# Two experts at a time: a large and a small one take turns step by step, with a down product between gate and up

## The chip, the cores and the metric

The program runs on one core of one Trainium2 chip. The metric is device time in microseconds: the median of the kernel before is 1894.28 us over three runs (1891.65 to 1898.52). The core works with TensorE (matmuls), VectorE and ScalarE (elementwise work), GpSimd, and SyncE, which issues the loads from HBM. Each engine takes its own list of instructions in order; they wait for each other by semaphores.

## The reference, cut to what matters

Two transformer blocks over 256 tokens of width 1024. The last stage, where the change is, is a mixture of experts: a router picks 2 of 8 experts for each token, and every expert is a gated product with an inner width of 3584.

```python
logits = (hf @ w_router)
top_val, top_idx = lax.top_k(logits, 2)
gates = jax.nn.softmax(top_val, axis=-1)
...
def expert_block(args):
    xb, e = args
    return (jax.nn.silu(xb @ w_gate[e]) * (xb @ w_up[e])) @ w_down[e]
...
h = layer_norm(ALPHA * h + y, ln_g, ln_b)
```

Everything is float32, and the products keep nearly all of that accuracy.

## The kernel before, in words

A float32 product is made of products of a faster 4-byte format. Each weight is cut into a high part (ScalarE copies it into `WHB` or `WHX`, line 1290) and the rest (VectorE subtracts, into `WLB` or `WLX`, line 1911). The rows are cut the same way. An expert with up to 128 tokens ("large") needs three matmuls for each pair of tiles: high by high, high by low, low by high (`mm3`, lines 442 to 444). For an expert with at most 64 tokens ("small", `LIGHT`) high and low rows stand side by side in one operand of 128 columns, so two matmuls do (lines 1093 and 1094, 1139 and 1140); its two halves are then added when the hidden rows are turned (`expert_turn`, line 1117: 16 small matmuls, where a large expert has 4).

The experts are ranked by their load, and the table `RANK` says which rank stands at which position. Before, positions 0, 3 and 6 are large and the others small, and one expert is done after the other.

The weights of one expert are 21 loads of 2 MB: for each of its seven chunks of 512 inner columns one of gate, up and down. SyncE issues them in the order of the list `WL_M`, into four slots (three of `ring`, and `ring4`); a slot is loaded again once VectorE has cut its contents. Each load is cut in two halves ("pieces"), 42 an expert. The cut parts have four places. ScalarE cuts four pieces ahead of TensorE (`split_to(done + 3)`, line 1276) and VectorE three ahead (line 1904); the fourth place comes free only when TensorE has used up the piece in it. In between, the same two engines take the results from PSUM, at fixed points of their lists.

The seven chunks are done in steps of one or two (`steps_of`, line 38). A step is, on TensorE: gate products of this step's chunks; after their first piece the turn of the first chunk of the step before; up products, and among them the turn of its second chunk; then the down products of the chunks of the step before. PSUM banks are fixed: gate in 0 and 1, up in 2 and 3, down in 4 and 5, the turn in 6, all else in 7 (`LAST_BANK` for the last sums). Among these stand the gathering of the next expert's rows (`gather`, line 1056), its lists (`scatter_lists`) and the sums of the last expert into the tokens' rows (`combine`, line 1175). After the last expert come its sums, a layer norm (lines 2650 and 2655) and the stores.

Of the kernel before, what the change touches and what calls it, by code (L numbers as in the profile page):

```python
# [8 lines left out]
F32 = mybir.dt.float32  # L9
# [23 lines left out]
RANK = (0, 3, 4, 1, 5, 6, 2, 7)  # L33
LIGHT = (1, 2, 4, 5, 7)
# [88 lines left out]
def build(nc, I, table, out):  # L123
    ctx = ExitStack()
    with ctx:
# [16 lines left out]
        VS = sb("VS", [128, 256])  # L142
# [3 lines left out]
        BC = sb("BC", [128, 2, D])  # L146
        NG = sb("NG", [128, 128])
        GM = sb("GM", [128, 2, 64])
        LAMB = sb("LAMB", [128, 256])
# [20 lines left out]
        with ExitStack() as part:  # L170
# [18 lines left out]
            CT2 = pt("CT2", [128, 192])  # L189
        P8 = ctx.enter_context(nc.psum_tensor("PS", [128, 4096], F32))  # L190
# [33 lines left out]
        T = {}  # L224
# [46 lines left out]
        for ex in range(NE):  # L271
            for cs in steps_of(ex):
                for kind in ("gate", "up"):
                    if len(cs) == 2:
                        WL_M += [(f"{kind} {ex}", (CH * cs[0], 4 * k), None, 4, 2 * CH) for k in range(2)]
                    else:
                        WL_M.append((f"{kind} {ex}", (CH * cs[0], 0), None, 8, CH))
                WL_M += held
                held = [(f"down {ex}", 4 * c, None, 4, D) for c in cs]
# [144 lines left out]
        def pe_program(e):  # L424
# [631 lines left out]
            def gather(ex, q):  # L1056

                pe.wait_ge(s_po, ex + 1)
                light = ex in LIGHT
                for n, src in enumerate((HH, HL)):  # L1060
                    pe.wait_ge(*((s_hl, 2) if n else (s_hh, 2)))
                    b = 6 + (q if light else n)
                    if not (light and n):
                        room(b)
                    for j in range(4):
                        d = 4 * q + j
                        for tt in range(2):
                            if light:
                                at_ = 128 * j + 64 * n
                                t = e.matmul(PS[b][:, at_:at_ + 64], src[:, tt, 128 * d:128 * d + 128], PO[:, tt, 0:64], start=(tt == 0), stop=(tt == 1))  # L1070
                            else:
                                t = e.matmul(PS[b][:, 128 * j:128 * j + CAP], src[:, tt, 128 * d:128 * d + 128], PO[:, tt, :], start=(tt == 0), stop=(tt == 1))  # L1072
                    if n or not light:
                        t.then_inc(banks.put(("ga", ex, q, n), b), 1)

            def expert_piece(kind, ex, cs, k):
# [3 lines left out]
                at_ = 0 if kind == "gate" else 2  # L1080
# [4 lines left out]
                for j in range(n_kt):  # L1085
                    kt = n_kt * k + j
                    for x, c in enumerate(cs):
                        b = at_ + (NCH * ex + c) % 2
# [3 lines left out]
                        if ex in LIGHT:  # L1092
                            e.matmul(PS[b][:, :], EH[:, kt, :], wh, start=(kt == 0), stop=False)  # L1093
                            t = e.matmul(PS[b][:, :], EH[:, kt, :], wl, start=False, stop=(kt == 7))  # L1094
# [3 lines left out]
                if k == 2 * len(cs) - 1:  # L1098
                    for c in cs:
                        banks.put((kind, ex, c), at_ + (NCH * ex + c) % 2, full=used)  # L1100
# [6 lines left out]
            def expert_turn(ex, c):  # L1107
                n = NCH * ex + c
                i = n % 2
                room(6)  # L1110
                if ex in LIGHT:
                    pe.wait_ge(s_tab2, 16)
                    for x, (kind, src) in enumerate((("gate", HID[:, i, :]), ("up", UB[:, :]))):
                        pe.wait_ge(*banks.out[kind, ex, c])
                        for j in range(4):
                            at_ = 256 * x + 64 * j
                            t = e.matmul(PS[6][:, at_:at_ + 64], inner(src, j), CT2[:, 128:192], start=True, stop=True)
                else:
                    pe.wait_ge(*banks.out["up", ex, c])
                    for j in range(4):  # L1120
                        t = e.transpose(PS[6][:, 128 * j:128 * j + 128], inner(HID[:, i, :], j), ident)
# [2068 lines left out]
```

## Time and profile before

| what | value |
|---|---|
| median of three runs | 1894.28 us |
| the profiled execution's span | 1894.2 us |
| TensorE busy | 1833.4 us (97%) |
| weight loading into TensorE busy | 1524.4 us (80%) |
| VectorE busy | 1469.6 us (78%) |
| ScalarE busy | 1213.1 us (64%) |
| read from HBM | 508.98 MB, 269 GB/s over the span |
| loads of expert weights | 168 of 2048 KB, medians 10.9 to 11.7 us from issue to landing |

The profiled execution's own time is taken as its span; it is 0.1 us from the median. A busy TensorE in the page is one with matmuls in its pipeline: the records overlap (each lasts 0.39 us, and the next starts 0.23 us after it), so a share near 100% can hide short waits. VectorE's records overlap a little too. The stage of the experts takes from 989 us to the end, nearly half of the span.

### The profile page before, as it was taken

To read this page: it belongs to the slowest core of one execution; us is meant where nothing else is said; L and a number is where in the kernel's file an instruction comes from. 1 tells how busy PE (TensorE), PEld (TensorE's weight loads), DVE (VectorE), ACT (ScalarE), POOL (GpSimd) and SP (SyncE) were. 2 spreads that over 40 slices of the span, in tenths; PEclk is the share of its full clock that TensorE was granted. 3 is DMA by queue.
4 is the path that set the end of the run, shared out by engine and by line. 5 is a ranking of instruction groups with operands and counts; after the bars stand their busy time and mean duration, and the time that the engine had idled before them with its cause. 6 is when DMAs were issued, how large, how long until landed. Compare 5 with 4: busy or idle time off the path is not lost.

```text
span 1894.2 us, 22429 instructions
## 1 busy us (share of the span) xinstructions
PE 1833.4 (97%) x9190; PEld 1524.4 (80%) x9190; DVE 1469.6 (78%) x1418; ACT 1213.1 (64%) x1258; POOL 142.4 (8%) x118
## 2 busy tenths in 40 slices
PE   7999999999999999999999999999999999999997
PEld 6888878888988788888788887878888787888875
DVE  5646565444579764458879899999989999998997
ACT  6555555433564454345637788988778898777784
POOL 2511100000100140004130000000000000000000
PEclk9999999999999999999989999999999999999999
DMA  8533345544442465344358999999999999999994
GB/s 296 177 134 134 134 154 204 198 178 151 170 169 89 156 224 198 134 160 154 131 202 342 373 354 423 420 422 420 395 363 362 419 420 422 418 379 368 370 420 167
DMA packets 154782, 511.54 MB, mean 270 GB/s; under 512 B 4431, under 2 KB 8898, under 8 KB 140338
## 3 DMA queue, kind: packets, MB, share of 16 engines
q1 hardware_dynamic: 152674, 504.53, 69.2%
q0 software_dynamic: 1392, 4.53, 0.7%
q8 instruction: 74, 1.21, 0.2%
q10 hardware_dynamic: 608, 0.99, 0.1%
q14 instruction: 34, 0.28, 0.0%
HBM read 508.98 MB, written 1.05 MB: 269 GB/s over the span
## 4 chain that ended last, share of the span: by engine, by line
PE 71%; DVE 17%; DMA 6%; ACT 3%; issue 2%; POOL 0%; ACTq 0%; SPq 0%; DVEq 0%; POOLq 0%
PE PS L442 19%; PE PS L444 19%; PE PS L443 19%; DVE WLX L1911 6%; DVE WLB L1911 6%; DMA ring<-in_moe_w_down 4%; PE PS L900 2%; PE PS L1139 1%; PE PS L1140 1%; ACT WHX L1290 1%; DMA ring<-in_moe_w_gate 1%; PE PS L1070 1%; PE PS L1072 1%; ACT WHB L1290 1%; PE PS L596 1%
## 5 line engine op out<-in xcount | busy, mean ns | idle before, releaser
L1911 DVE TENSOR_TENSOR WLB<-ring,WHB 128x2048 fp32r<-128x2048 f32 (+1 forms) x344 | 636.6, 1867 | 113.2 <-ACT WHB L1290 112.7
L1290 ACT ACTIVATE WHB<-ring 128x2048 fp32r<-128x2048 f32 (+1 forms) x344 | 531.5, 1557 | 300.1 <-PE PS L444 270.6
L1911 DVE TENSOR_TENSOR WLX<-ring,WHX 128x2048 fp32r<-128x2048 f32 (+1 forms) x216 | 469.1, 2192 | 51.2 <-ACT WHX L1290 51.0
L1290 ACT ACTIVATE WHX<-ring 128x2048 fp32r<-128x2048 f32 (+1 forms) x216 | 392.6, 1834 | 156.4 <-PE PS L444 124.8
L442 PE MATMUL PS<-WHB,XH 128*128 128x512 f32 (+1 forms) x640 | 255.2, 399 | 8.6 <-DVE XL L1945 2.4
L444 PE MATMUL PS<-WHB,XL 128*128 128x512 f32 (+1 forms) x640 | 247.7, 387 | 0.0
L443 PE MATMUL PS<-WLB,XH 128*128 128x512 f32 (+1 forms) x640 | 247.1, 386 | 0.0
L442 PEld LDWEIGHTS PS<-WHB,XH 128*128 128x128 f32 x640 | 121.1, 189 | 36.7 <-issue 6.2
L2831 POOL TENSOR_TENSOR SM<-SM,MH 128x8 f32<-128x8 f32 (+3 forms) x28 | 38.1, 1366 | 1392.1 <-DVE SM L1924 1392.1
L444 PEld LDWEIGHTS PS<-WHB,XL 128*128 128x128 f32 x640 | 120.8, 189 | 25.0
L443 PEld LDWEIGHTS PS<-WLB,XH 128*128 128x128 f32 x640 | 121.3, 190 | 21.8
L1093 PE MATMUL PS<-WHX,EH 128*128 128x512 f32 x280 | 113.5, 405 | 2.8 <-DVE WLX L1911 2.1
L1093 PE MATMUL PS<-WHB,EH 128*128 128x512 f32 x280 | 112.8, 403 | 2.7 <-DVE WLB L1911 2.0
L1094 PE MATMUL PS<-WLX,EH 128*128 128x512 f32 x280 | 109.5, 391 | 0.0
L1094 PE MATMUL PS<-WLB,EH 128*128 128x512 f32 x280 | 109.4, 391 | 0.0
L442 PE MATMUL PS<-WHX,XH 128*128 128x512 f32 (+1 forms) x240 | 91.0, 379 | 1.4 <-DVE WLX L1911 1.4
L444 PE MATMUL PS<-WHX,XL 128*128 128x512 f32 (+1 forms) x240 | 90.1, 375 | 0.0
L443 PE MATMUL PS<-WLX,XH 128*128 128x512 f32 (+1 forms) x240 | 90.0, 375 | 0.0
L442 PE MATMUL PS<-WHB,HTH 128*128 128x512 f32 x184 | 72.2, 392 | 0.0
L443 PE MATMUL PS<-WLB,HTH 128*128 128x512 f32 x184 | 71.6, 389 | 0.0
L444 PE MATMUL PS<-WHB,HTL 128*128 128x512 f32 x184 | 71.6, 389 | 0.0
L1093 PEld LDWEIGHTS PS<-WHX,EH 128*128 128x128 f32 x280 | 52.6, 188 | 20.7 <-DVE WLX L1911 10.6
(422 smaller groups left out, 3407.6 us busy)
## 6 DMA issues: line engine op xcount, KB each, us to landing
ring<-in_moe_w_gate SPq DMA_DIRECT2D x56, 2048.0 KB, 11.1
ring<-in_moe_w_up SPq DMA_DIRECT2D x56, 2048.0 KB, 10.9
ring<-in_moe_w_down SPq DMA_DIRECT2D x56, 2048.0 KB, 11.7
ring<-in_w_in SPq DMA_DIRECT2D x13, 2048.0 KB, 7.8
ring<-in_hg_w_in SPq DMA_DIRECT2D x8, 2048.0 KB, 8.4
ring<-in_da_w_in SPq DMA_DIRECT2D x6, 2048.0 KB, 7.9
ring<-in_w_gate SPq DMA_DIRECT2D x5, 2048.0 KB, 7.5
ring<-in_w_up SPq DMA_DIRECT2D x5, 2048.0 KB, 7.6
```

Source lines behind the costliest of these rows:

```text
L442: e.matmul(o, xh, wh, start=start, stop=False)
L443: e.matmul(o, xh, wl, start=False, stop=False)
L444: return e.matmul(o, xl, wh, start=False, stop=stop)
L596: t = e.matmul(PS[4 + q][:, dv * h:dv * h + dv], PTBUF[a][h % 2][:, 128 * j:128 * j + 128], VR[VK[a]][:, k, dv * h:dv * h + dv], start=(k ...
L900: t = e.matmul(PS[b][:, 128 * j:128 * j + 128], a_k[:, h, 128 * s_t:128 * s_t + 128], a_q[:, h, 128 * t_t:128 * t_t + 128], start=True, st ...
L1070: t = e.matmul(PS[b][:, at_:at_ + 64], src[:, tt, 128 * d:128 * d + 128], PO[:, tt, 0:64], start=(tt == 0), stop=(tt == 1))
L1072: t = e.matmul(PS[b][:, 128 * j:128 * j + CAP], src[:, tt, 128 * d:128 * d + 128], PO[:, tt, :], start=(tt == 0), stop=(tt == 1))
L1093: e.matmul(PS[b][:, :], EH[:, kt, :], wh, start=(kt == 0), stop=False)
L1094: t = e.matmul(PS[b][:, :], EH[:, kt, :], wl, start=False, stop=(kt == 7))
L1290: e.activation(hi, src, ACT.Copy).then_inc(s_hi, 1)
L1911: e.tensor_tensor(lo, src, hi.bitcast(F32), ALU.subtract).then_inc(s_lo, 1)
L2831: e.tensor_tensor(RR[name], RV[name], MH[:, 0:RR[name].shape[1]], ALU.pow).then_inc(s_rs, 1)
```

## The change

The table `RANK` puts the large experts at positions 0, 2 and 4. A written order, `ORDER`, lets two experts run at the same time, a step of each in turn: position 0 with 1, 1 with 2, and so on, up to 5 with 6; the last steps are of small experts alone. In a step of two chunks the down product of the first held chunk stands between the gate and the up products, and the loads follow in the same order. The turn of the first held chunk stands ahead of the gate products (from the fourth step on), that of the second in their middle. Rows, place lists, copied up products and down sums exist twice, for the odd and the even expert (`EHB`, `POB`, `POTB`, `UBB`, and banks 3 to 6 for down sums); four banks (0, 1, 7, 2) go round for everything else (`turns`). The second set of rows lies where the norm's vectors `BC` were, so the vectors for the last norm are loaded only after the last expert's rows have been read. ScalarE and VectorE follow the same order with their parts.

```diff
-RANK = (0, 3, 4, 1, 5, 6, 2, 7)
-LIGHT = (1, 2, 4, 5, 7)
+RANK = (0, 3, 1, 4, 2, 5, 6, 7)
+LIGHT = (1, 3, 5, 6, 7)
 HEAVY = NE - len(LIGHT)
 
 
-def steps_of(ex):
-
-    return ((0, 1), (2, 3), (4, 5), (6,)) if ex == NE - 1 else ((0,), (1, 2), (3, 4), (5, 6))
+def chunks_of(ex, s):
+
+    return (((0, 1), (2, 3), (4, 5), (6,)) if ex == NE - 1 else ((0,), (1, 2), (3, 4), (5, 6)))[s]
+
+
+ORDER = (0, 0, 1, 0, 1, 0, 1, 2, 1, 2, 3, 2, 3, 2, 3, 4, 3, 4, 5, 4, 5, 4, 5, 6, 5, 6, 6, 7, 6, 7, 7, 7)
+SEQ = [(ex, chunks_of(ex, ORDER[0:n].count(ex))) for n, ex in enumerate(ORDER)]
+BEGIN = [ORDER.index(ex) for ex in range(NE)]
+END = [len(ORDER) - 1 - ORDER[::-1].index(ex) for ex in range(NE)]
+CHUNK = [(ex, c) for ex, cs in SEQ for c in cs]
+IDX = {x: m for m, x in enumerate(CHUNK)}
+LISTED = {BEGIN[ex] - 2: ex for ex in range(1, NE)}
+GATHERED = {BEGIN[ex] - 1: ex for ex in range(1, NE)}
+SCATTERED = {4: 0, 5: 1, 12: 2, 13: 3, 20: 4, 21: 5, 28: 6, 29: 7}
+COMBINED = {END[ex] + 2 + i: (ex, 2 * i) for ex in range(NE - 1) for i in range(2)}
+LAST = len(SEQ) - 1
...
+        POTS = [POT, sb("POTB", [128, 2, 128], FR)]
...
+        EHB = sb("EHB", [128, 8, CAP], FR)
+        PLACES = [PO, sb("POB", [128, 2, CAP], FR)]
...
+        UBB = sb("UBB", [128, CH])
...
+        ROWS, UBS = [EH, EHB], [UB, UBB]
...
+        for ex, cs in SEQ:
+            two = len(cs) == 2
+            for kind in ("gate", "up"):
+                if two:
+                    WL_M += [(f"{kind} {ex}", (CH * cs[0], 4 * k), None, 4, 2 * CH) for k in range(2)]
+                    if kind == "gate":
+                        WL_M += held[0:1]
+                        held = held[1:]
+                else:
+                    WL_M.append((f"{kind} {ex}", (CH * cs[0], 0), None, 8, CH))
+            WL_M += held
+            held = [(f"down {ex}", 4 * c, None, 4, D) for c in cs]
         WL_M += held
...
+            turns = [0, 1, 7, 2]
+
+            def take():
+                b = turns.pop(0)
+                room(b)
+                return b
+
...
+                if k == 0:
+                    for c in cs:
+                        BANK[kind, ex, c] = turns.pop(0)
...
+                        turns.append(BANK[kind, ex, c])
...
+            def between_products(n, i):
+
+                if n in COMBINED and i in (0, 2):
+                    ex, k = COMBINED[n]
+                    combine(ex, k + i // 2)
+                if n in SCATTERED and i == 1:
+                    scatter_lists(SCATTERED[n])
+                if n in GATHERED:
+                    ex = GATHERED[n]
+                    if ex not in LIGHT:
+                        gather(ex, i // 2, i % 2)
+                    elif i % 2:
+                        gather(ex, i // 2, 1)
 
             for q in range(2):
+                for x in range(2):
+                    gather(0, q, x, (6, 7, 3, 2)[2 * q + x])
+            for n, (ex, cs) in enumerate(SEQ):
+                held = [(SEQ[n - 1][0], c) for c in SEQ[n - 1][1]] if n else []
+                two, held_two = len(cs) == 2, len(held) == 2
+                n_p = 2 * len(cs)
+                if n > 2:
+                    expert_turn(*held[0])
+                for k in range(n_p):
+                    expert_piece("gate", ex, cs, k)
+                    if n in (1, 2) and k == 0:
+                        expert_turn(*held[0])
+                    if held_two and k == n_p // 2 - 1:
+                        expert_turn(*held[1])
+                between_products(n, 0)
+                if two:
+                    if held:
+                        expert_down(*held[0])
+                    between_products(n, 1)
+                for k in range(n_p):
+                    expert_piece("up", ex, cs, k)
+                    if k == n_p // 2 - 1:
+                        between_products(n, 2 if two else 1)
+                if not two:
+                    between_products(n, 2)
+                    if held:
+                        expert_down(*held[0])
+                between_products(n, 3)
+                if n == LAST:
+                    expert_turn(ex, cs[0])
+                if held_two:
+                    expert_down(*held[1])
...
+            p.wait_ge(*T["e read", NE - 1])
+            p.wait_ge(*banks.full["sl", NE - 1])
```

Two places of it, as the instructions stand. TensorE, where one step of a small expert ends and the next step begins; before, from the last down products (the small matmuls of line 1117 are the turn, `HTH` the turned rows, `EH` the gathered rows):

```order
L1139 MATMUL PS<-WHX1,HTH 128x512
L1140 MATMUL PS<-WLX1,HTH 128x512
L1093 MATMUL PS<-WHB0,EH 128x512 [waits s_out0,s_lo]
L1094 MATMUL PS<-WLB0,EH 128x512
L1093 MATMUL PS<-WHB0,EH 128x512 [waits s_out1]
L1094 MATMUL PS<-WLB0,EH 128x512
L1093 MATMUL PS<-WHB0,EH 128x512
L1094 MATMUL PS<-WLB0,EH 128x512
L1093 MATMUL PS<-WHB0,EH 128x512
L1094 MATMUL PS<-WLB0,EH 128x512
L1117 MATMUL PS<-CT2,HID 128x64 x4
L1117 MATMUL PS<-CT2,UB 128x64 [waits s_out2]
L1117 MATMUL PS<-CT2,UB 128x64 x3
```

After, at the ninth step's end and the tenth's start (lines 1134 and 1135 are the small expert's products, 1161 the turn, 470 to 472 a large expert's products):

```order
L1135 MATMUL PS<-WLB1,EHB 128x512
L1134 MATMUL PS<-WHB1,EHB 128x512
L1135 MATMUL PS<-WLB1,EHB 128x512
L1161 MATMUL PS<-CT2,HID 128x64 [waits s_add]
L1161 MATMUL PS<-CT2,HID 128x64 x3
L1161 MATMUL PS<-CT2,UBB 128x64 [waits s_out2]
L1161 MATMUL PS<-CT2,UBB 128x64 x3
L470 MATMUL PS<-WHX0,EH 128x512 [waits s_add,s_lo]
L471 MATMUL PS<-WLX0,EH 128x512
L472 MATMUL PS<-WHX0,EL 128x512
```

The turn now stands right behind the last up product, where before a down product and a piece of gate products lay between. In two-chunk steps whose held step also has two chunks, one down product still lies there.

ScalarE at the same kind of place; before (1290 cuts weights, 1773 copies up products, 1783 and 1790 take the turned rows):

```order
L1290 ACTIVATE WHB0<-ring 128x2048 [waits s_used,s_ring2]
L1290 ACTIVATE WHB1<-ring 128x2048 [waits s_used]
L1773 ACTIVATE UB<-PS 128x512
L1290 ACTIVATE WHX0<-ring 128x2048 [waits s_used,s_ring0]
L1290 ACTIVATE WHX1<-ring 128x2048 [waits s_used]
L1290 ACTIVATE WHB0<-ring 128x2048 [waits s_used,s_ring1]
L1783 ACTIVATE SGT<-PS 128x256 [waits s_htl,s_full6]
L1290 ACTIVATE WHB1<-ring 128x2048 [waits s_used]
L1790 ACTIVATE HTH<-SGT 128x4x64 [waits s_ub]
```

After (1357 cuts weights, 1843 copies up products, 1854 and 1861 take the turned rows):

```order
L1357 ACTIVATE WHX0<-ring4 128x2048 [waits s_used,s_ring3]
L1357 ACTIVATE WHX1<-ring4 128x2048 [waits s_used]
L1357 ACTIVATE WHB0<-ring 128x2048 [waits s_used,s_ring2]
L1357 ACTIVATE WHB1<-ring 128x2048 [waits s_used]
L1843 ACTIVATE UBB<-PS 128x512
L1843 ACTIVATE UB<-PS 128x512
L1854 ACTIVATE SGT<-PS 128x256 [waits s_htl,s_full1]
L1357 ACTIVATE WHX0<-ring 128x2048 [waits s_used,s_ring0]
L1861 ACTIVATE HTH<-SGT 128x4x64 [waits s_ub]
```

The copies of the up products of both chunks now stand together, with the taking of the first turned rows right behind them.

## Rows read from the trace of the kernel before

**Rows 1.** The page's rate of transfers in 40 slices of the span, GB/s.
```profile
GB/s 296 177 134 134 134 154 204 198 178 151 170 169 89 156 224 198 134 160 154 131 202 342 373 354 423 420 422 420 395 363 362 419 420 422 418 379 368 370 420 167
```

**Rows 2.** Stretches (us): PE, PEld, DVE, ACT, POOL busy, PEclk, DMA share, GB/s.
```profile
1020.00:1080.00 60.00, 60.00 (x276) 49.90 (x276) 53.38 (x33) 43.77 (x28) 0.00 (x0) 1.00 0.98 383
...
1186.00:1291.00 105.00, 100.94 (x500) 81.04 (x499) 102.71 (x67) 91.43 (x75) 0.00 (x0) 1.00 1.02 422
1360.00:1440.00 80.00, 80.00 (x382) 67.08 (x381) 68.86 (x44) 58.12 (x40) 0.00 (x0) 1.00 0.95 360
```

**Rows 3.** Timeline of SyncE, weight loads: start us, us, line, operation.
```profile
1074.99 0.40 SPq L3001 DMA_DIRECT2D ring<-in_moe_w_gate  x1
...
1186.10 0.37 SPq L3001 DMA_DIRECT2D ring<-in_moe_w_gate  x1
...
1290.75 0.37 SPq L3001 DMA_DIRECT2D ring<-in_moe_w_gate  x1
...
1405.82 0.37 SPq L3001 DMA_DIRECT2D ring<-in_moe_w_gate  x1
...
1738.68 5.30 SPq L3001 DMA_DIRECT2D ring<-in_moe_w_gate  x2
```

**Rows 4.** Timeline of TensorE in a large expert: start us, us.
```profile
1000.04 0.39 PE L442 MATMUL PS<-WHX,EH 128*128 128x512 f32 x1
...
1004.58 0.40 PE L444 MATMUL PS<-WHB,EL 128*128 128x512 f32 x1
...
1005.20 0.47 PE L442 MATMUL PS<-WHB,EH 128*128 128x512 f32 x1
```

**Rows 5.** Timeline of TensorE in small experts: gather, then turn.
```profile
1200.03 1.06 PE L1070 MATMUL PS<-PO,XL 128*128 128x64 f32 x8
1200.92 0.48 PE L1139 MATMUL PS<-WHX,HTH 128*128 128x512 f32 x1
...
1861.08 1.16 PE L1117 MATMUL PS<-CT,HID 128*128 128x64 f32 x8
1862.07 1.10 PE L1117 MATMUL PS<-CT,UB 128*128 128x64 f32 x8
1862.98 0.48 PE L1139 MATMUL PS<-WHX,HTH 128*128 128x512 f32 x1
```

**Rows 6.** Timeline of VectorE in a large expert.
```profile
1004.09 4.47 DVE L1911 TENSOR_TENSOR WLX<-ring,WHX 128x2048 fp32r<-128x2048 f32 x2
1008.50 0.67 DVE L2622 TENSOR_TENSOR HTL<-PS,HTH 128x512 fp32r<-128x512 f32 x1
1009.10 4.47 DVE L1911 TENSOR_TENSOR WLB<-ring,WHB 128x2048 fp32r<-128x2048 f32 x2
```

**Rows 7.** Groups of VectorE from 960 us: busy, mean ns, idle before.
```profile
L1911 DVE TENSOR_TENSOR WLB<-ring,WHB 128x2048 fp32r<-128x2048 f32 x168 | 381.0, 2285 | 11.2 <-ACT WHB L1290 10.9
...
L2615 DVE TENSOR_TENSOR SGT<-PS,SGT 128x256 f32<-128x256 f32 x35 | 14.7, 421 | 4.0 <-ACT SGT L1783 3.6
```

**Rows 8.** Waits from 1186 to 1291 us: total, times, longest.
```profile
PEld PS L1093 <- DVE WLX L1911: 3.7, 6, 1.1
```

**Rows 9.** Waits from 1020 to 1080 us.
```profile
ACT WHX L1290 <- PE PS L444: 8.2, 11, 1.1
```

**Rows 10.** Timeline of ScalarE in a small expert.
```profile
1857.92 1.91 ACT L1290 ACTIVATE WHX<-ring 128x2048 fp32r<-128x2048 f32 x1
...
1860.03 0.59 ACT L1773 ACTIVATE UB<-PS 128x512 f32<-128x512 f32 x1
```

**Rows 11.** Timelines of TensorE and VectorE at the stage's ends; one issue.
```profile
989.51 0.73 PE L442 MATMUL PS<-WHB,EH 128*128 128x512 f32 x1
...
1877.96 0.39 PE L1140 MATMUL PS<-WLX,HTH 128*128 128x512 f32 x1
...
1884.04 1.41 DVE L2650 SCALAR_TENSOR_TENSOR LZ<-PS,SM,BC 128x512 f32<-128x512 f32 x2
...
BC<-in_ln_b POOLq DMA_DIRECT2D x4, 512.0 KB, 5.2
```

More of the change, by code:

```diff
@@ L1054, in pe_program, with gather @@
             go_on(6, 2)
-            def gather(ex, q):
+            turns = [0, 1, 7, 2]
[3 more added lines that the diff above has]
+                return b
+            def gather(ex, q, n, b=None):
                 pe.wait_ge(s_po, ex + 1)
                 light = ex in LIGHT
[L1060 to L1064, printed above, removed]
+                if b is None:
+                    b = take()
+                    turns.append(b)
+                else:
+                    room(b)
+                for i, src in enumerate((HH, HL)):
+                    if not light and i != n:
+                        continue
+                    pe.wait_ge(*((s_hl, 2) if i else (s_hh, 2)))
                     for j in range(4):
@@ L1107, in expert_turn @@
             def expert_turn(ex, c):
-                n = NCH * ex + c
-                i = n % 2
-                room(6)
+                m = IDX[ex, c]
+                i = m % 2
+                b = take()
+                turns.append(b)
+                BANK["mt", ex, c] = b
                 if ex in LIGHT:
                     pe.wait_ge(s_tab2, 16)
-                    for x, (kind, src) in enumerate((("gate", HID[:, i, :]), ("up", UB[:, :]))):
+                    for x, (kind, src) in enumerate((("gate", HID[:, i, :]), ("up", UBS[i][:, :]))):
                         pe.wait_ge(*banks.out[kind, ex, c])
@@ L1175, in combine @@
             def combine(ex, k):
                 tt, q = k // 2, k % 2
-                b = 7
+                b = take()
+                turns.append(b)
+                BANK["cb", ex, k] = b
                 cs = slice(512 * q, 512 * q + 512)
-                room(b)
                 pe.wait_ge(s_zl, 2 * ex + q + 1)
                 pe.wait_ge(s_pot, 2 * ex + 1)
-                e.matmul(PS[b][:, :], POT[:, tt, :], ZH[:, cs], start=True, stop=False)
-                e.matmul(PS[b][:, :], POT[:, tt, :], ZL[:, cs], start=False, stop=True).then_inc(banks.put(("cb", ex, k), b, out=(s_add, 4 * ex + k + 1)), 1)
@@ L1215, in pe_program @@
             rows_first(0)
             rows_first(2)
-            expert_down(*before[0])
+            expert_down(ex, cs[0])
             rows_first(1)
@@ L2700, in dve_program @@
                     pieces_done()
-                    if before:
-                        expert_turned(*before[0], 1)
-                    if two:
+                between_products(n, 0)
+                if two:
+                    if held:
                         pieces_done(2)
-                    if ex and s in (1, 2):
-                        combined(ex - 1, 2 * s - 2)
-                    if s == 3:
-                        scatter_lists(ex)
-                        if more:
-                            lists(ex + 1)
@@ L2741, in dve_program @@
+                if held and not two:
+                    pieces_done(2)
+                between_products(n, 3)
+                if n == LAST:
+                    for stage in range(2):
+                        expert_turned(ex, cs[0], stage)
+                if held_two:
+                    pieces_done(2)
+                if held and held[-1][1] == NCH - 1:
+                    down_out(held[0][0])
             pieces_done(2)
```

382 lines of the change are left out of this document (183 added, 199 removed).

## Prediction

> **What bounds the kernel now.** I read the page's rate of transfers first, since half of the program is one long stream of weights. From slice 25 on the reader is to see a pattern that comes three times: some four slices at 418 to 423 GB/s, then some three at 342 to 396 [rows 1]. So the stream is at its limit in some stretches only. The view by stretches says which: in a small expert (1186 to 1291 us) the DMA share is 1.02, VectorE is busy for 102.7 of 105 us and TensorE's records leave gaps; in a large one (1020 to 1080, 1360 to 1440) TensorE has no gap at all, the rate is 383 and 360, and VectorE has room [rows 2]. The waits agree: in the small expert TensorE waits for VectorE's low parts [rows 8], in the large one ScalarE waits for TensorE to give a place free [rows 9]. The clock is granted in full in all of these, so it plays no part.
>
> The issues of the loads then give lengths. From one small expert's first gate load to the next one's is 1290.75 − 1186.10 = 104.65 us; from position 1 to position 4 it is 330.8, from there to position 7 332.9 [rows 3]. Less two small ones, a large expert takes 121.5 to 123.6.
>
> Now each engine's own demand, from the pitch at which it works without waiting.
>
> TensorE: 20 matmuls from 1000.04 to 1004.58, so 0.227 us each; a large turn adds 1005.20 − 1004.58 − 0.23 = 0.39 [rows 4]. A large expert has 42 pieces × 12 = 504 matmuls, 114.4 us; 7 turns, 2.7. The gather of 32 small matmuls goes at 0.89 us for 8 [rows 5], 3.5; combining is 8 × 0.227 = 1.8; the six matmuls of the lists at the gather's pitch, 0.7. Together 123.1. A small one: 42 × 8 = 336 matmuls, 76.3; a turn takes 1862.98 − 1861.08 = 1.9 [rows 5], seven are 13.3; and the same 6.0. Together 95.6.
>
> VectorE: two cuts and the start of what follows take 4.41 us, 2.205 each, and a copy from PSUM 0.60 [rows 6]. An expert's 42 cuts are 92.6. A large one adds 14 products of 0.60 (HID, HTL), 8.4; a small one 14 of 128x256, recorded 0.42 [rows 7] and so some 0.35 apart, 4.9; both some 5 for sums, places and lists. Large 106, small 102.5. The stream: 21 × 2.097 MB = 44.0 MB at 422 GB/s [rows 2], 104.3 us.
>
> So large experts are bound by TensorE (123 against 106 and 104), small ones by the stream and VectorE together (104.65 against 95.6 of TensorE). Each small expert leaves TensorE 9 us idle; five make 45. That is all that the change can win, since it takes away no instruction.
>
> At this point the Trainium skill speaks against the change. The row of the small expert shows 422 GB/s [rows 2]. "DMA: Bandwidth & Descriptors", section "Where 436 GB/s comes from", says that for transfers between HBM and SBUF the HBM side, some 358 GB/s a core, is what binds. By that an estimated 123 us would be needed for any expert, TensorE's idle time could not be filled, and the time would stay. The trace does not agree, and the row decides.
>
> **The change, part by part.**
>
> *The mixing of steps.* Up to the last large step, the new order has 22 steps with all 21 large chunks and 17 small ones; then come 10 steps with the other 18 small chunks alone. Mixed part: TensorE 21/7 × 123.1 + 17/7 × 95.6 = 369.3 + 232.2 = 601.5 us; VectorE 3 × 106 + 17/7 × 102.5 = 567; the stream 38/7 × 104.3 = 566. TensorE is the bound there by 34 us. Does the lead carry it over from a large to a small step? A large step of two chunks has 8 large pieces (2.72 each), 4 small down pieces (1.82) and two small turns: 32.8 us; VectorE needs 12 × 2.205 + 2.6 = 29.1. A small step: 8 × 1.82 + 4 × 2.72 + 0.8 = 26.3; VectorE 26.5 + 1.2 = 27.7. It falls back 1.4 us, with two sums and their like some 3, against three cut pieces of lead, 6.6 us. It carries, and the swapped downs help: they bring large down pieces into small steps. The small rest: 18/7 × 104.65 = 269.1 us. Sum 870.6.
>
> By the same sum the kernel before is 3 × 123.1 + 5 × 104.65 = 892.6, and the trace has 1877.96 − 989.51 + 0.23 = 888.7 from the first expert matmul to the last down product [rows 11]. The 3.9 less are the lead that TensorE eats up at three borders from large to small; the new order has one such border, 1.3. So 869.3 against 888.7: 19.4 us won if nothing new waits.
>
> At VectorE a rule and a row can be weighed. Its cuts are recorded at 2.285 us [rows 7], yet follow each other at 2.205 [rows 6]. "VectorE: DVE Perf Modes", section "The TRN2 errata", gives (N+151)/0.96 ns for such an operation, 2.291 us at 2048 elements. By that an estimated 96.2 us of cuts would make a small expert 106, more than the 104.65 that it takes; the mixed part would be at some 588, still under TensorE. The record agrees with the rule, but the pitch is what adds up, and the sum goes by it.
>
> *The turn ahead of the gate products.* It needs the up product copied out. ScalarE first cuts the piece whose place the last up matmul gave free, and then copies: 1.9 + 0.59 us [rows 10], with two hand-overs 2.7. Where a down product lies between (3.6 us small, 5.4 large) that is hidden. Where the held step has one chunk nothing lies there: five places in the mixed part (steps 4, 9, 12, 17, 20, counted from 0). Two have small held chunks: the turn's first half (1 us) goes meanwhile, 1.7 is left, so 3.4. Three have large ones, where VectorE's product follows at once: 0.67, the time of the other one of that size [rows 6], and two hand-overs, some 0.9 each, 2.7. Behind the turn the whole of TensorE is queued. The bounds for an exposed turn are 0 (the wait is made good by VectorE's larger lead later) and 2.7. I take 6 in all, nearest to the rows. In the small rest one more such place is in time that the stream owns.
>
> *Banks that go round.* A gate product takes the bank of an up product that was emptied before the turn could run, and combines and gathers take banks a whole product old. I find none at which a wait must show, and bound it by 0 and one PSUM copy of 0.6 us in 32 steps, 19. I take 2, nearest to the row of the large expert, where TensorE never waits for a bank [rows 2].
>
> *Second sets of rows and lists.* They allow the gather to be early and cost no instruction. The norm's vectors are now loaded after the last up product, near 1861 [rows 5]; such a load takes some 5 us [rows 11] and is needed at 1884.04 [rows 11]. Hidden by 15 us; if not, the end would slip by what is over.
>
> *Down between gate and up.* It moves two pieces in front of four in the same queue of loads and cuts. TensorE needs the turned rows four gate pieces after the turn: 7.3 us at the least, against a chain of a gate piece (1.8), a cut (1.9 [rows 10]) and two small operations (0.4 each), some 4.5. No cost.
>
> Sum: −19.4 + 6 + 2 = −11.4: 1894.2 − 11.4 = 1882.8, say 1883. The profiled execution is 0.1 us from the median, so this is also the median's forecast.
>
> **Rivals.**
>
> A. Nothing new shows. TensorE runs the mixed part without a gap as it does in large experts now [rows 2]. Against it: five places with nothing between up and turn. 1894 − 19 = 1875.
>
> B. VectorE becomes the bound in the mixed part. It waits for turned rows and up products at fixed points of its list, and the lead is only three pieces. If no lead carries over, a large step of two takes TensorE's 32.8 + 1.7 us (its share of gathers and sums), a small one VectorE's 27.7 + 2.5, a pair 64.7 against 2/7 × (123.1 + 104.65) = 65.1 now; 8.5 pairs win 3.4, two borders' lead (2.6) is lost and the exposed turns of large chunks cost 3: 1896. For it: the lead of 6.6 us is short. Against it: the mixed sums above leave 34 us.
>
> C. The turn is exposed at every step, not at five: because ScalarE runs late behind its copies, or the going round of banks holds the turn. With w us in each of 29 steps it is 1894.2 − 19.4 + 29 w. It is slower than the kernel before by more than can be told from w = 0.86 on; at the full 1.7 it is 1924, at 1.0 1904. For it: TensorE's list is strict, and all is behind the turn. Against it: the down product hides 3.6 us of 2.7.
>
> D. The stream is the bound everywhere, so that mixing gives nothing and the rate reads the same in both kinds of step: 1894. The skill's rule of "DMA: Bandwidth & Descriptors" above would do this; against it stand the two rates in rows 2.
>
> **How the numbers follow.** A measurement of this kernel tells 0.3%, 5.7 us, from no change. Forecast 0.40, A 0.25, B 0.18, C 0.13, D 0.04. Faster than 1888.6: 0.33 of the forecast, all of A, and 0.02 each of B and C, 0.62. Same: 0.07 of the forecast, 0.13 of B, 0.03 of C, and D, 0.27. Slower: 0.03 of B and 0.08 of C, 0.11. The range is from 1868, where the small rest too gains a little, to 1898, which takes in B and the mild end of C; C's rest and the very low end are left out.
>
> **What would show it.** Right: no dips to 342 to 396 GB/s in the mixed part but an even rate near 395 (38 × 6.29 MB in some 605 us); TensorE without gaps until some 1600 us, and VectorE near 95% busy all along; then 422 GB/s until the end; first to last expert matmul some 877 us. Turns in steps 9 and 17 with a wait for ScalarE's copy. Wrong: gaps of TensorE in small steps of the mixed part that end with low parts (B), or a wait at each turn (C); an even rate of 422 with idle TensorE (D).

## The result, and the profile after

The changed kernel takes 1909.82 us (median of 4 runs, 1907.45 to 1911.52), the one before, measured beside it, 1895.66 us (median of 4 runs, 1891.65 to 1898.52). The ratio is 1.0075, with a 95% interval of 1.0063 to 1.0086: it is slower, by some 14 us, where 1883 us was forecast. The time lies outside the range of 1868 to 1898. The profiled execution has a span of 1909.2 us.

The page first. Busy times are nearly those of before, so no work was added; the rates are what [rows 1] was.

```profile
PE 1837.9 (96%) x9190; PEld 1531.7 (80%) x9190; DVE 1469.4 (77%) x1418; ACT 1212.2 (63%) x1258; POOL 142.5 (7%) x118
GB/s 295 174 133 133 133 169 206 197 155 177 173 136 89 176 221 180 150 176 133 160 141 363 378 393 393 396 338 381 389 391 394 358 377 385 401 413 412 423 421 203
```

The pattern of [rows 1] is gone, as forecast, and in the small rest the rate goes up to 423. But the mixed part stands at 338 to 396, not near 395. The view by stretches (TensorE, its weight loads, VectorE, ScalarE, GpSimd busy; granted clock; DMA share; GB/s) answers to [rows 2]:

```profile
1020.00:1080.00 60.00, 60.00 (x293) 50.62 (x293) 51.44 (x28) 44.96 (x33) 0.00 (x0) 1.00 0.96 368
1080.00:1110.00 30.00, 27.63 (x122) 22.60 (x121) 27.00 (x18) 23.97 (x17) 0.00 (x0) 0.94 0.96 379
1200.00:1260.00 60.00, 56.00 (x266) 46.25 (x264) 51.75 (x32) 43.88 (x34) 0.00 (x0) 0.97 0.98 384
1290.00:1320.00 30.00, 27.63 (x118) 22.57 (x117) 26.55 (x17) 20.82 (x14) 0.00 (x0) 0.95 1.01 409
1440.00:1470.00 30.00, 27.83 (x130) 23.05 (x130) 26.95 (x19) 21.03 (x17) 0.00 (x0) 0.94 1.01 412
1530.00:1560.00 30.00, 27.63 (x119) 22.50 (x118) 26.33 (x17) 22.90 (x16) 0.00 (x0) 0.94 0.95 375
1680.00:1710.00 30.00, 27.18 (x125) 21.93 (x123) 26.67 (x17) 23.54 (x20) 0.00 (x0) 0.94 1.01 415
1020.00:1600.00 580.00, 564.83 (x2692) 470.52 (x2692) 521.79 (x328) 447.95 (x333) 0.00 (x0) 0.99 0.97 380
```

The reader is to see two things. TensorE loses 2 to 4 us in each of six short stretches, and in the same six, and only there between 1000 and 1890 us, the granted clock is below 1. The rest of the mixed part is not free of gaps either, and VectorE is busy for 522 of 580 us, 90%, not 95%.

What ends TensorE's pauses is in the waits from 1000 to 1600 us (total, times, longest):

```profile
DVE HTH L2689 <- ACT HTH L1861: 29.9, 17, 3.5
PE PS L1166 <- DVE HID L2699: 8.7, 4, 2.4
PE PS L1161 <- ACT UBB L1843: 5.5, 2, 3.3
PEld PS L1134 <- DVE WLX L1977: 4.7, 6, 1.1
PE PS L1134 <- DVE WLX L1977: 2.1, 4, 0.7
PEld PS L470 <- DVE WLX L1977: 1.7, 4, 0.7
PEld PS L1134 <- DVE WLB L1977: 1.4, 4, 0.4
```

Lines 1166 and 1161 are the turn, of a large and of a small chunk. It waits at the places that the prediction named (steps 4, 9, 12, 17 and 20 in the mixed part, one more in the rest), but for 2.2 to 3.3 us each and not 0.9 or 1.7. The fourth wait of line 1166 stands at none of them: it is 1.58 us before the very first turn, at 1006.5 us, where the kernel before does not wait. The first of the named ones, on TensorE, VectorE and ScalarE:

```profile
1081.50 0.39 PE L472 MATMUL PS<-WHX,EL 128*128 128x512 f32 x1
1084.26 0.72 PE L1166 MATMUL PS<-CT,HID 128*128 128x128 f32 x4 [2.37 <-DVE HID L2699]
```

```profile
1076.56 4.49 DVE L1977 TENSOR_TENSOR WLB<-ring,WHB 128x2048 fp32r<-128x2048 f32 x2
1081.22 2.29 DVE L1977 TENSOR_TENSOR WLX<-ring,WHX 128x2048 fp32r<-128x2048 f32 x1 [0.17 <-ACT WHX L1357]
1083.43 1.28 DVE L2699 TENSOR_TENSOR HID<-PS,HID 128x512 f32<-128x512 f32 x2
```

```profile
1079.27 1.92 ACT L1357 ACTIVATE WHX<-ring 128x2048 fp32r<-128x2048 f32 x1 [0.86 <-PE PS L472]
```

The last up matmul starts at 1081.50. VectorE's product `HID`, for which the turn waits, starts only at 1083.43, since a cut stands before it in its list, and that cut began at 1081.22, when ScalarE had made its high part. In a small chunk ScalarE is late. Two cuts, and not one, stand ahead of its copy of `UBB`, and the first of them has waited for its load:

```profile
1223.33 3.71 ACT L1357 ACTIVATE WHB<-ring 128x2048 fp32r<-128x2048 f32 x2 [1.21 <-DMA ring<-in_moe_w_gate]
1226.94 0.58 ACT L1843 ACTIVATE UBB<-PS 128x512 f32<-128x512 f32 x1
```

The turn there starts its second half at 1227.57, after a wait of 3.29 us. The other two small places look the same: two cuts of 3.71 us together, after waits of 1.05 and 1.28 us for a load.

From the first expert matmul to the last down product the stage takes 989.5 to 1893.3 us, 903.8 us, where 877 was forecast and 888.7 was measured before. The small rest, counted from 1624.9 us, where the first down product of the last large step ends, takes 268.4 us against 269.1 forecast: all of the error is in the mixed part, to within the 2 us by which the border between the two can be drawn otherwise.

### The profile page after: what moved, and what is told of

Read it like the earlier page. It is cut to its first block, busy times and chain, and to the rows that moved or that the text cites. A ratio compares the mean times of both kernels' runs of the same rounds, so it can differ in the third digit from the quotient of the medians.

```text
span 1909.2 us, 22486 instructions
## 1 busy us (share of the span) xinstructions
PE 1837.9 (96%) x9190; PEld 1531.7 (80%) x9190; DVE 1469.4 (77%) x1418; ACT 1212.2 (63%) x1258; POOL 142.5 (7%) x118
## 3 DMA queue, kind: packets, MB, share of 16 engines
q8 instruction: 75, 1.23, 0.2%
HBM read 508.98 MB, written 1.05 MB: 267 GB/s over the span
## 4 chain that ended last, share of the span: by engine, by line
PE 73%; DVE 17%; DMA 3%; ACT 3%; issue 3%; POOL 0%; ACTq 0%; SPq 0%; DVEq 0%; POOLq 0%
PE PS L470 18%; PE PS L472 18%; PE PS L471 18%; DVE WLB L1977 6%; DVE WLX L1977 5%; PE PS L1134 3%; PE PS L1135 3%; DMA ring<-in_moe_w_gate 2%; PE PS L1161 2%; ACT WHB L1357 2%; PE PS L928 2%; PE PS L1185 1%; PE PS L1186 1%; PE PS L1109 1%; PE PS L1111 1%
## 5 line engine op out<-in xcount | busy, mean ns | idle before, releaser
L1134 PE MATMUL PS<-WHX,EHB 128*128 128x512 f32 x224 | 91.1, 407 | 3.8 <-DVE WLX L1977 3.6
L1134 PE MATMUL PS<-WHB,EHB 128*128 128x512 f32 x224 | 92.8, 414 | 1.6 <-DVE WLB L1977 1.3
L1135 PE MATMUL PS<-WLB,EHB 128*128 128x512 f32 x224 | 90.5, 404 | 0.0
L1135 PE MATMUL PS<-WLX,EHB 128*128 128x512 f32 x224 | 87.7, 392 | 0.0
```

The lines of the kernel that those rows point to most:

```text
L1134: e.matmul(PS[b][:, :], ROWS[ex % 2][:, kt, :], wh, start=(kt == 0), stop=False)
L1135: t = e.matmul(PS[b][:, :], ROWS[ex % 2][:, kt, :], wl, start=False, stop=(kt == 7))
```

## The experiments

Theory 1: the exposed turns make the change slower, each by its wait and by the slower clock behind it. Theory 2: mixing wins next to nothing even without them, since VectorE falls behind in small pieces.

**The down product of a lone chunk goes back behind up.** Loads, cuts and matmuls alike, so that it lies between the up products and the next step's turn:

```diff
-                    if held:
-                        expert_down(*held[0])
+                if held and not (two and held_two):
+                    expert_down(*held[0])
```

> Only where the held step has one chunk (seven places), its down product goes back behind the up products, so that it lies between the last up product and the next turn. All else is as in the changed kernel (1909.8 us). Theory 1, the exposed turn: in the trace after, six turns right behind the last up product wait 2.3 to 3.4 us each, and the granted clock is at half for 3.4 us after each of them, some 4.4 us a place; with the down product between, all six vanish: 1909.8 - 26 = 1884, at most 1889. Theory 2, the lead of three pieces is too short for mixed steps (VectorE starves TensorE in many small waits, and the exposed turns only show it): the time moves by less than 7 us, 1903 or more.

Measured: 1897.97 us, ratio 1.0017 (1.0008 to 1.0027), granted clock 0.992. It gives back 12 us, between the two theories, which had 21 or more and under 7. The clock is full from 1000 to 1870 us and none of the named turns waits, but another wait comes in, TensorE for ScalarE's copy of a gate product whose bank comes round: the term "Banks that go round", which I had put at 2 us in all.

```profile
PE PS L1134 <- ACT HID L1836: 3.1, 2, 1.6
PE PS L470 <- ACT HID L1836: 2.7, 2, 1.4
```

**All down products behind up**, with the same edit for every step.

> All down products go back behind the up products; the mixed order of experts stays, and so do turn and banks. Theory 1: every turn has one or two down products in front of it, so it gives the same as the kernel with the lone down moved, within 4 us, 1884 to 1890. Theory 2: the down products between gate and up are what evens out large and small steps; without them the lead runs out more, and it is slower than the kernel with the lone down moved by 5 us or more.

Measured: 1914.23 us, 1.01 (1.0083 to 1.0116). Slower than the kernel with the lone down product moved by 16 us, as theory 2 had it, but not for its reason alone: here TensorE waits for that copy 25 us in all, in many places. So the down product between gate and up is not by itself what loses: with banks that go round it hides this wait.

```profile
PE PS L1131 <- ACT HID L1831: 18.9, 14, 2.2
PE PS L467 <- ACT HID L1831: 6.1, 5, 1.4
```

**One expert after the other**, everything else as in the change.

```diff
-ORDER = (0, 0, 1, 0, 1, 0, 1, 2, 1, 2, 3, 2, 3, 2, 3, 4, 3, 4, 5, 4, 5, 4, 5, 6, 5, 6, 6, 7, 6, 7, 7, 7)
-SCATTERED = {4: 0, 5: 1, 12: 2, 13: 3, 20: 4, 21: 5, 28: 6, 29: 7}
+ORDER = tuple(n // 4 for n in range(32))
+SCATTERED = {END[ex]: ex for ex in range(NE)}
```

> The mixed order alone is undone: one expert after another (large ones at positions 0, 2 and 4), with the new banks, the turn ahead of the gate products and the down product between gate and up as in the changed kernel. Theory 1: mixing itself wins what was forecast (19 us) and the rest of the change costs some 30; so this one is slower than the changed kernel by 10 to 19 us, 1920 to 1929. Theory 2, mixing is what costs: it is at 1905 or below.

Measured: 1910.7 us, 1.008 (1.0063 to 1.0097), as much as the change, and in neither theory's range. As long as the turns are exposed, mixing neither wins nor loses that can be told; the loss is there without any mixing, and seven turns wait in this trace too, for 1.4 to 3.5 us.

**The waits filled.** Five matmuls of 256 columns, whose results nobody reads, stand in each exposed turn's wait.

```diff
+            def filler(b):
+                for _ in range(5):
+                    e.matmul(PS[b][:, 256:512], ident, CT[:, 0:256], start=True, stop=True)
```

> The changed kernel with five matmuls of 256 columns, whose result is overwritten, inside each wait of the exposed turns, so that TensorE is not idle there; they fit in the wait (some 2.1 us of 2.3 to 3.4). If the half clock after each exposed turn comes from TensorE's pause before it, the six stretches at half clock vanish and the time is 1909.8 - 10 = 1900. If the clock falls for another reason, it stays at 1909 to 1912.

Measured: 1900.83 us, 1.0032 (1.002 to 1.0045), 9 us less than the change with more work in it. The clock is full in the stretches where it was not:

```profile
1080.00:1110.00 30.00, 29.88 (x142) 24.73 (x140) 28.79 (x18) 25.41 (x19) 0.00 (x0) 1.00 1.00 398
1530.00:1560.00 30.00, 29.88 (x139) 24.69 (x138) 28.30 (x19) 23.43 (x16) 0.00 (x0) 1.00 0.97 381
```

**Copies first.** ScalarE and VectorE take the gate and up products out of PSUM one cut earlier. No instruction is added, only moved:

```diff
-                    pieces_done(2)
+                    pieces_done()
+                    for c in cs:
+                        expert_up(ex, c)
+                    pieces_done()
```

> TensorE's list, the loads and the banks are those of the changed kernel. Only ScalarE and VectorE take the finished gate and up products one cut earlier in their lists, so that the copy that an exposed turn waits for no longer stands behind a cut of 1.9 (ScalarE) or 2.3 us (VectorE). Theory 1, the wait is made of that cut: the waits at the turn fall from 2.3 to 3.4 us to 1.3 or less, no clock falls after them, and the kernel wins about what the filled one won and half the waits, 1909.8 - 10 - 8 = 1892. Rival: the wait is the copies' own latency and the lead, and a cut put off starves TensorE as much right after: less than 4 us won, 1906 or more.

Measured: 1894.79 us, 1.0004 (0.9994 to 1.0013). 15 us of the change's time are gone, or 13.5 counted by the two ratios, 1.0075 and 1.0004. The clock is full from 1020 to 1600 us, and the three large turns still wait, 0.88 us each. The product now starts at 1080.15, ahead of the cut:

```profile
1080.15 1.29 DVE L2702 TENSOR_TENSOR HID<-PS,HID 128x512 f32<-128x512 f32 x2 [0.49 <-PE PS L472]
1081.35 2.28 DVE L1980 TENSOR_TENSOR WLX<-ring,WHX 128x2048 fp32r<-128x2048 f32 x1
```

```profile
1080.00:1110.00 30.00, 29.12 (x141) 24.16 (x140) 29.85 (x19) 26.50 (x19) 0.00 (x0) 1.00 1.01 405
1020.00:1600.00 580.00, 573.22 (x2752) 475.33 (x2752) 534.05 (x339) 460.93 (x340) 0.00 (x0) 1.00 0.99 390
```

What is left on TensorE from 1000 to 1600 us is mainly the weight loads that wait for VectorE's low parts, 12.8 us in 24 places:

```profile
PEld PS L1134 <- DVE WLX L1980: 5.3, 6, 1.1
PEld PS L1134 <- DVE WLB L1980: 4.1, 9, 0.7
PEld PS L470 <- DVE WLX L1980: 2.8, 7, 0.7
PEld PS L1185 <- DVE WLX L1980: 0.6, 2, 0.3
```

**Two combinations and one part alone.** The lone down product behind up, together with copies first:

> As the last one, with the lone down product moved behind the up products too (1898.0 by itself). In the trace of that kernel the turns no longer wait, but four matmuls wait 1.6 us for ScalarE's gate copy, since their bank comes round a product earlier. If these and the low parts that come late are what is left, it wins 6 us or more on 1898, 1886 to 1892. If what is left is VectorE's pace, it stays within 3 us of 1898.

Measured 1898.23, 1.0016 (1.0007 to 1.0026): the two don't add, and the time is that of the second reading, within 3 us of 1898. The change, with ScalarE copying the second half of the turned rows directly after the first, since VectorE waited 29.9 us for such copies (`expert_turned(*held[0], 1)` moves up one cut):

> The changed kernel; only ScalarE makes the second copy of the turned rows right behind the first and not after its next cut. In the trace after, VectorE waits 30 us in the mixed part (17 times, up to 3.5 us) for that copy, which stands behind a cut that itself waits for TensorE. Theory, this eats the lead of three pieces and so what mixing should win: 5 us or more won, 1904 or less. Rival: TensorE is the bound there and VectorE's waits are idle time that costs nothing: within 3 us of 1909.8.

Measured 1908.18, 1.0064 (1.0042 to 1.0086): the largest wait in VectorE's list cost less than can be told. All three:

> The lone down product behind the up products, copies of gate and up products one cut earlier, and the turned rows' copy at once, together. By the sum of the three theories: 1909.8 - 12 - 8 - 5 = 1885, faster than the kernel before (1895). If mixing wins nothing on this chip, it ends at 1893 to 1898.

Measured 1897.97, 1.0017 (1.0007 to 1.0026), at the end of the range for mixing that wins nothing. And copies first with the second half at once:

> The change with early copies, and ScalarE copies both halves of the turned rows directly one after the other. VectorE waits less for turned rows. If these waits are what keeps TensorE idle in the mixed part: 1886 to 1889. If they cost next to nothing, as the run with only this edit showed (1.7 us): 1893 to 1895.

Measured 1894.06, 0.9997 (0.9987 to 1.0007), the kernel before's time. VectorE's 21.6 us of waits for that copy (1020 to 1600 us) are gone from the trace, and TensorE's waits for low parts are the same to 0.2 us: it was not these waits that made the low parts late.

**Mixing by itself.** One expert after the other, with copies first, so that no turn is exposed by much in either order:

> One expert after the other (large at 0, 2 and 4), everything else of the change kept, and ScalarE and VectorE take gate and up products one cut earlier. No step is mixed, and no turn should be exposed by more than some 1.3 us. Against the mixed order with the same early copies (1894.8) this is the price of mixing alone. If mixing is worth the 19 us of the forecast and they are won there: some 1913. If the gain of mixing does not come even without exposed turns: 1896 to 1899, so 2 to 4 us over the mixed order.

Measured 1893.88, 0.9996 (0.9987 to 1.0006), against 1.0004 (0.9994 to 1.0013) for the mixed order. Mixing is worth nothing that can be told, and not 19 us. The time is below both ranges: even without mixing, the change with early copies takes what the kernel before takes.

**VectorE's cuts halved**, in the kernel before and in the mixed order with copies first:

```diff
+                    if n >= FIRST["M"]:
+                        lo, src, hi = lo[:, 0:1024], src[:, 0:1024], hi[:, 0:1024]
```

> The kernel before, in which VectorE cuts only half the columns of each piece of expert weights, so the low parts of the other half are not computed (the output is not the reference's). VectorE's 336 cuts get some 1.07 us shorter. It is then no bound anywhere; small experts are bound by the stream alone at 104.3 us instead of 104.65, large ones by TensorE as now. Where the stream bounds small experts: 1888 to 1893. Where VectorE's pace and lead did: down to 1880. It is the base for the mixed order with the same half cuts.

> The change with early copies, and VectorE cuts only half the columns of each piece of expert weights, as in the run of the kernel before with half cuts. Theory 1, VectorE's pace and its lead of three pieces eat what mixing should win: with half cuts the mixed order reaches 1875 to 1880, at least 10 us below the kernel before with half cuts. Rival, the gain is lost elsewhere (the stream, the banks, the order of TensorE itself): it stays within 4 us of that kernel, near 1890.

Measured: 1890.72, 0.998 (0.9967 to 0.9992), and 1882.13, 0.9937 (0.9914 to 0.996). The clean comparison is the mixed order with copies first, whole cuts against half: 1894.79 to 1882.13, 12.7 us won, and no weight load of TensorE waits for a low part any more in the waits from 1000 to 1600 us, where it had been 12.8 us. From the first expert matmul to the end of the last large down product the stage takes 636.9 us with whole cuts and 627.4 with half, so 9.5 us are won in the mixed part and the rest in the small steps. Against the kernel before with half cuts the mixed order is now 8.6 us faster. That kernel has the old banks and the old place of the turn; one expert after the other with copies first and half cuts was not run, so the 8.6 us are not shown to be mixing alone. In both the clock is full from 1020 to 1600 us:

```profile
1020.00:1600.00 580.00, 563.96 (x2752) 469.19 (x2751) 326.90 (x348) 476.80 (x365) 0.00 (x0) 1.00 1.00 400
```

```profile
1020.00:1600.00 580.00, 574.80 (x2788) 483.63 (x2788) 324.75 (x344) 466.18 (x346) 0.00 (x0) 1.00 0.99 395
```

The first row is the kernel before, the second the mixed order. The even 395 GB/s of the prediction comes true here, with half of VectorE's cuts gone; at that rate the mixed part's loads take the 605 us that it had. Where the time goes with whole cuts is seen in the mixed order with copies first, where a large step ends and small pieces follow. TensorE's weight loads, then VectorE:

```profile
1144.71 0.19 PEld L1134 LDWEIGHTS PS<-WHB,EHB 128*128 128x128 f32 x1 [0.65 <-DVE WLB L1980]
1149.72 0.19 PEld L1134 LDWEIGHTS PS<-WHX,EHB 128*128 128x128 f32 x1 [1.00 <-DVE WLX L1980]
```

```profile
1138.58 1.29 DVE L2702 TENSOR_TENSOR HID<-PS,HID 128x512 f32<-128x512 f32 x2 [0.79 <-PE PS L472]
1139.79 2.28 DVE L1980 TENSOR_TENSOR WLB<-ring,WHB 128x2048 fp32r<-128x2048 f32 x1
1141.98 0.48 DVE L2623 TENSOR_SCALAR PO<-CT,SM 128x128 fp32r<-128x128 f32 x2
1142.38 2.28 DVE L1980 TENSOR_TENSOR WLB<-ring,WHB 128x2048 fp32r<-128x2048 f32 x1
1144.58 2.28 DVE L1980 TENSOR_TENSOR WLX<-ring,WHX 128x2048 fp32r<-128x2048 f32 x1
1146.78 0.68 DVE L2695 TENSOR_TENSOR HTL<-PS,HTH 128x512 fp32r<-128x512 f32 x1
1147.38 2.28 DVE L1980 TENSOR_TENSOR WLX<-ring,WHX 128x2048 fp32r<-128x2048 f32 x1
```

VectorE waits 0.79 us for the up product, and then works without a pause: from 1138.58 to 1149.58 four cuts, two products, two instructions for a list and a `HTL`, 11.0 us for four pieces, where TensorE needs 1.82 for a small one. Whatever lead there was is spent, and the small pieces wait 0.65 and 1.00 us.

**GpSimd takes a part of each cut**, 256 or 512 of 2048 columns, in the mixed order with copies first and in the kernel before (there 512). VectorE's cut of a piece now waits until GpSimd's part of it is done:

```diff
+            for n in range(FIRST["M"] + 8, PIECE_END):
+                src, hi, lo = piece(n)
+                p.wait_ge(s_hi, n + 1)
+                e.tensor_tensor(lo[:, 1536:2048], src[:, 1536:2048], hi[:, 1536:2048].bitcast(F32), ALU.subtract).then_inc(s_tail, 1)
```

> The change with early copies; GpSimd, idle in this stage, cuts the last 256 of 2048 columns of each piece, VectorE the other 1792. Theory 1, VectorE's time starves TensorE in the mixed part: the cut gets 0.27 us shorter, 2.205 to 1.94 by its width, so VectorE needs 567 - 228 x 0.27 = 505 us for the mixed part, and most of what half cuts won comes: 1886 to 1889. Rival, the two engines get in each other's way or the hand-over is late: 1893 or more.

> As before, with 512 columns for GpSimd and 1536 for VectorE. Theory 1: VectorE's cut takes 1.67 us, GpSimd's part, of which no row here shows a time, fits beside it: 1883 to 1886, near the 1882.1 of half cuts. Rival: GpSimd's part takes longer than a piece has or holds VectorE up: 1895 to 1930, with VectorE waiting for GpSimd.

> The kernel before, with GpSimd cutting 512 of 2048 columns of each piece. If both can work at once it is near the kernel before with half cuts, 1890 to 1893, and at least 5 us over the mixed order with the same share. If they hinder each other it is slower than before.

Measured: 1927.84 (1.0173, 1.0156 to 1.019), 1989.63 (1.0494, 1.0476 to 1.0511) and 1982.12 (1.0457, 1.044 to 1.0475). The rivals held, and by more than their ranges in the second run. VectorE's cuts with 256 columns given away, and GpSimd's:

```profile
1200.26 2.03 DVE L1986 TENSOR_TENSOR WLB<-ring,WHB 128x1792 fp32r<-128x1792 f32 x1 [0.64 <-POOL WLB L3061]
1202.91 2.55 DVE L1986 TENSOR_TENSOR WLB<-ring,WHB 128x1792 fp32r<-128x1792 f32 x1 [0.63 <-POOL WLB L3061]
1205.38 2.55 DVE L1986 TENSOR_TENSOR WLX<-ring,WHX 128x1792 fp32r<-128x1792 f32 x1
```

```profile
1200.47 2.41 POOL L3061 TENSOR_TENSOR WLB<-ring,WHB 128x256 fp32r<-128x256 f32 x1 [0.24 <-ACT WHB L1359]
1202.84 0.74 POOL L3061 TENSOR_TENSOR WLX<-ring,WHX 128x256 fp32r<-128x256 f32 x1
1204.08 1.97 POOL L3061 TENSOR_TENSOR WLX<-ring,WHX 128x256 fp32r<-128x256 f32 x1 [0.51 <-ACT WHX L1359]
```

Whichever starts first makes the other last longer. The cut of 1200.26 starts before GpSimd's instruction and takes 2.03 us, and GpSimd's lasts 2.41, past the cut's end. The cuts of 1202.91 and 1205.38 start while one of GpSimd's is under way and take 2.55, more than a whole cut's 2.28. On average from 1020 to 1600 us a cut with 256 columns given away takes 2.12 to 2.15 us, a little less than the whole cut's 2.28, but VectorE now waits 63 us for GpSimd; with 512 given away it takes 2.33 to 2.39, more than a whole one, and waits 58.5 us. So the loss is made of the hand-over and of the longer instructions, and no run parts the two. That a lighter VectorE helps with all the work done is so not shown; that a later one costs at once is.

## Why the prediction was wrong

The error in the stage is 903.8 − 877.3 = 26.5 us. The runs divide it in two: the change costs 1909.8 − 1894.8 = 15.0 us that copies first gives back, where the terms for turns and banks had 8; and mixing, forecast at −19.4, is worth nothing. 15.0 − 8 + 19.4 = 26.4. That this comes out so near says little, since the kernel with copies first takes the time of the one before; what shows that mixing is worth nothing is the run with one expert after the other.

1. *"The turn ahead of the gate products"*, forecast +6: mis-sized, and the step that gave the result its sign. The places were right. The price was not: 2.2 to 3.3 us a place, 12.5 us in the five of the mixed part. For a large chunk I had VectorE stand ready at its product, while a cut of 2.28 us stands ahead of it, and this cut had itself waited for ScalarE's; what is left of the cut when TensorE is done, and the first product, make the 2.37 us. For a small chunk I had one cut of ScalarE ahead of the copy, and there were two, held back by a late load. And I took the clock as having no part. Behind each of these pauses it was half for some 3.4 us (30 us at 0.94), 1.7 us lost each; filling the pauses gave back 9 us. The net cost is less than waits and clock together (21 us in the mixed part): the run with copies first has 15 us.

2. *"The mixing of steps", "It carries, and the swapped downs help"*: −19.4 did not come. The sum of demands was near: TensorE is the bound on the mean, by 34 us, and with half cuts the stream runs at the rate that the sum had. The step that failed is "It carries". I let 6.6 us of lead be there at each border and be spent by 1.4 us a step. In fact TensorE's weight loads wait for low parts, 12.8 us from 1000 to 1600 us with copies first, and half cuts take these waits away and win 12.7 us, 9.5 of them in the mixed part. In the small pieces VectorE's 2.205 us a cut, with copies and lists between, stands against 1.82. That it also enters them without its full lead, having waited for the up product (0.79 us above), fits the rows, but no run tries it by itself. Of the rest of the 19.4 us, 2.6 are the three large turns' waits; where the remainder lies stays open. This is rival B's mechanism, with C's exposed turns on top, at five places and one and not at all 29. That B had 1896 for its time, and copies first gave 1894.8, is partly luck: B let VectorE set the pace of every small step, and the trace has 24 waits of at most 1.1 us. Neither rival alone gave 1910; B's 1896, which holds 3 us of exposed turns, and the 15 us come to 1908 to 1911.

3. *"Banks that go round"*, +2: no such wait in the change itself. With the lone down product moved behind up it shows, 1.4 to 1.6 us at four places of the mixed part, and 25 us in all where every down stands behind up.

4. *Second sets, down between gate and up, the small rest*: as forecast. The rest took 268.4 for 269.1 us; the norm's vectors were asked for at 1879 us and first used at 1899. One number of the prediction is wrong by its own terms, and nothing rests on it: with 2.291 us a cut, VectorE's mixed part is 586.5 us and not 588.

5. *The range*, 1868 to 1898, took in B and the mild end of C, each alone, and left out both together, though both come from ScalarE and VectorE being late.

Still open: whether it is VectorE's pace or only its lead of three pieces. Half cuts change both. A fifth place for cut pieces would tell them apart; it was not tried. And the kernel before itself gained some 4 us by half cuts (0.998, 0.9967 to 0.9992), so its small experts too had waited a little for VectorE, and its 104.65 us was not the stream's alone.

No version that does all the work beat the kernel before by more than can be told: the best two, one expert after the other with copies first and the mixed order with copies first and both halves of the turned rows at once, take 1893.88 and 1894.06 us, 0.9996 and 0.9997 of it.

## What to carry to other kernels

Two demands that fit on the mean don't overlap by that: look whether the engine with less slack really enters its hard stretch with its lead, or has just waited at a fixed point of its list. Price an exposed hand-over by what stands in front of the producer in its own list, and that by what it waits for. When a new order exposes one, moving the copy ahead of the next large instruction is worth at least as much as hiding it (15 us here, against 12 for the down product in between).

## What the hardware showed unexpectedly

*Short pauses can cost clock, and not each does.* In the changed kernel TensorE, busy on both sides, paused at the six exposed turns for 2.2 to 3.3 us, and after each of these pauses the granted clock stood at the lower level, 1.2 GHz, for some 3.4 us (0.94 over 30 us). Cheap matmuls in the pause kept it at 2.4 GHz: 1909.8 to 1900.8 us. The pause's length alone does not decide. In the change with the turned rows copied at once, two pauses of 2.37 us (at 1082 and 1543 us) were followed by 2.4 GHz, and so were two with one expert after the other (at 1260 and 1492 us). With copies first, the three pauses of 0.88 us cost no clock, but one of 1.25 us inside a small turn did (0.83 from 1670 to 1680 us). In the kernel before the clock is at 0.91 from 1620 to 1640 us, where a wait of 1.23 us lies just ahead of the gather's small matmuls. What decides is open; a forecast can only give such a pause a chance of costing 1.7 us.

*GpSimd and VectorE.* A VectorE cut of 1792 columns took 2.03 us, and 2.55 when it started during one of GpSimd's of 256 columns; GpSimd's took 0.74 us when it started just ahead of VectorE's, and 1.97 to 2.41 when it started during one (the rows above, single instructions). The Trainium skill, "GPSIMD Engine Reference", section "Specifications", lists GpSimd's way to SBUF as shared with VectorE, with contention when VectorE has two SBUF inputs; the cut has two, and the trace agrees.
